# Causal mask of forgetting attention: added to the scores by a matrix product in PSUM instead of read from masked forget sums

## The reference, cut to what matters

```python
def fox_block(q, k, v, fq, fk, qpos, kpos):
    logits = jnp.einsum('bhqd,bhkd->bhqk', q, k).astype(jnp.float32) * (q.shape[-1] ** -0.5)
    logits = logits + fq[..., :, None] - fk[..., None, :]
    logits = jnp.where(qpos[:, None] >= kpos[None, :], logits, -jnp.inf)
    p = jax.nn.softmax(logits, axis=-1)
    return jnp.einsum('bhqk,bhkd->bhqd', p.astype(v.dtype), v)
...
fcum = jnp.cumsum(logf, axis=-1)   # fk: running sum of the log forget values
```

## Time and profile before

| | |
|---|---|
| median of 3 runs | 3345.48 us (3340.01, 3345.48, 3346.04) |
| profiled execution, its own time | 3339.98 us |
| its span, first to last instruction | 3338.2 us |
| PE busy | 3124.5 us, 94% |
| PEld, DVE, ACT, POOL busy | 85%, 42%, 30%, 28% |
| mean granted TensorE clock | 0.975 of full speed |
| the eight fox groups | four from 372 to 733 us, four from 2003 to 2371 us |

### The profile page before, as it was taken

How to read it: one execution, slowest core, us unless ns; L and a number is a source line. 1 busy time by engine, 2 the same in 40 slices (tenths; PEclk the granted TensorE clock), 3 DMA queues, 4 the chain that set the end, 5 groups by cost and what they waited for, 6 DMA issues and landing times. The chain is left out here.

```text
span 3338.2 us, 48224 instructions
## 1 busy us (share of the span) xinstructions
PE 3124.5 (94%) x20188; PEld 2853.0 (85%) x20188; DVE 1386.7 (42%) x2770; ACT 999.2 (30%) x1774; POOL 946.7 (28%) x536
## 2 busy tenths in 40 slices
PE   5899999999999999999989899999899999999996
PEld 2887877789999999999857787788799999999995
DVE  2412244455544463345152114444545354533532
ACT  3220433333334243221040223333324343331211
POOL 0121212215343443332111121221344352523320
PEclk9899999999999999999989999999999999999998
DMA  7112212212112121432432212222212121123334
GB/s 269 65 34 82 71 68 72 72 49 74 52 53 62 48 61 45 165 114 82 172 134 76 78 34 72 72 72 72 65 49 67 42 73 47 51 100 123 125 101 166
DMA packets 125560, 277.97 MB, mean 83 GB/s; under 512 B 44385, under 2 KB 64353, under 8 KB 124193
## 3 DMA queue, kind: packets, MB, share of 16 engines
q1 hardware_dynamic: 125344, 274.89, 24.3%
HBM read 217.24 MB, written 62.05 MB: 84 GB/s over the span
## 5 line engine op out<-in xcount | busy, mean ns | idle before, releaser
L272 PE MATMUL ps<-sb_h_split,sb_w_split 128*128 128x364 f32 (+1 forms) x3504 | 1232.9, 352 | 73.8 <-POOL sb_w_split L323 25.2
L273 PE MATMUL ps<-sb_h_split,sb_w_split 128*128 128x364 f32 (+1 forms) x3504 | 1163.5, 332 | 0.0
L274 PE MATMUL ps<-sb_h_split,sb_w_split 128*128 128x364 f32 (+1 forms) x3504 | 1162.7, 332 | 0.0
L272 PEld LDWEIGHTS ps<-sb_h_split,sb_w_split 128*128 128x128 f32 x3504 | 671.8, 192 | 104.6 <-issue 49.8
L273 PEld LDWEIGHTS ps<-sb_h_split,sb_w_split 128*128 128x128 f32 x3504 | 672.0, 192 | 6.5 <-issue 1.1
L274 PEld LDWEIGHTS ps<-sb_h_split,sb_w_split 128*128 128x128 f32 x3504 | 669.5, 191 | 0.0
L321 POOL CAST sb_w_split<-sb_w_raw 128x1024 fp32r<-128x1024 f32 x154 | 179.0, 1162 | 1710.8 <-PE ps L274 1630.1
L323 POOL TENSOR_TENSOR sb_w_split<-sb_w_raw,sb_w_split 128x1024 fp32r<-128x1024 f32 x154 | 387.1, 2514 | 12.3
L1444 PE MATMUL ps<-sb_delta 128*128 128x128 f32 x2160 | 263.0, 276 | 0.0
L1444 PEld LDWEIGHTS ps<-sb_delta 128*128 128x128 f32 x2160 | 258.4, 191 | 1.5
L1137 ACT ACTIVATE sb_fox<-sb_fox 128x128 f32<-128x128 f32 (+5 forms) x144 | 111.9, 777 | 328.0 <-DVE sb_fox L1172 327.7
(11 more groups left out here) (222 smaller groups left out, 4031.7 us busy)
## 6 DMA issues: line engine op xcount, KB each, us to landing
sb_w_raw<-in_wblk SPq DMA_DIRECT2D x158, 512.0 KB, 3.7
scratch_gates<-sb_spill SPq DMA_DIRECT2D x72, 182.0 KB, 1.9
sb_o_split<-scratch_o SPq DMA_DIRECT2D x24, 544.0 KB, 5.8
sb_fox<-scratch_fcum SPq DMA_DIRECT2D x8, 1600.0 KB, 6.7
sb_w_raw<-in_wbr SPq DMA_DIRECT2D x48, 256.0 KB, 3.9
sb_raw_qk<-scratch_gates SPq DMA_DIRECT2D x22, 544.0 KB, 3.7
sb_w_raw<-in_adaw SPq DMA_DIRECT2D x20, 512.0 KB, 15.8
sb_norm<-scratch_x SPq DMA_DIRECT2D x8, 1088.0 KB, 8.4
```

Of the source, the lines that this page charges most:

```text
L272: pe.matmul(out, w_hi, x_hi, start=first, stop=False)
L273: pe.matmul(out, w_hi, x_lo, start=False, stop=False)
L274: return pe.matmul(out, w_lo, x_hi, start=False, stop=last)
```

## The change

The mask now enters as one more product. The constant `causal` holds -8e30 for keys in the future, and after the scores of a tile are in PSUM, PE multiplies the identity by it and accumulates the result onto the diagonal block (times 0.125 it is -1e30). DVE then needs one operation for the whole row, with fk itself. POOL no longer makes fd.

```diff
-    causal = np.where(i[None, :] > i[:, None], 1e30, 0.0)
+    causal = np.where(i[None, :] > i[:, None], -8e30, 0.0)
...
             def _(pool):
-                pool.wait_ge(*hist_loaded(16))
-                for h in range(2):
-                    pool.tensor_tensor(fd[:, h, 0:8, :], Q4(fk[:, h, 0:SEQ]),
-                                       causal.unsqueeze(1).to_broadcast([P, 8, P]), ALU.add)\
-                        .then_inc(*level_mask.up(1))
-                    pool.tensor_tensor(fd[:, h, 8, 0:DEC], fk[:, h, SCAN_OFF:FKEYS], causal[:, 0:DEC],
-                                       ALU.add).then_inc(*level_mask.up(1))
                 split_blocks(pool, [3, 6, 9, 12])
...
-                                           kT[64 * h:64 * h + 64, lo + a:lo + a + w], start=True, stop=True)
+                                           kT[64 * h:64 * h + 64, lo + a:lo + a + w], start=True,
+                                           stop=(a + w < n))
+                    a, w = P * (len(blk) - 1), blk[-1][1]
+                    for h in range(2):
+                        r = 0 if t < 8 else DEC * h
+                        mm = pe.matmul(ps[0:rows, 2 * h + a // 512, a % 512:a % 512 + w],
+                                       ident[r:r + rows, r:r + rows], causal[r:r + rows, r:r + w],
+                                       start=False, stop=True)
                     mm.then_inc(*scores_pe.up(1))
...
-                    lo, w = blk[0][0], blk[-1][1]
-                    n = P * (len(blk) - 1)
+                    lo, n = blk[0][0], sum(b[1] for b in blk)
...
-                    if n:
-                        dve.tensor_tensor_reduce(out=lg[0:rows, s % 2, 0:n], in0=src[:, 0:n],
-                                                 in1=fk[0:rows, h, lo:lo + n], scale=0.125, scalar=-3e38,
-                                                 op0=ALU.subtract, op1=ALU.max,
-                                                 accum_out=mx[0:rows, s, 0:1])
-                    dve.tensor_tensor_reduce(out=lg[0:rows, s % 2, n:n + w], in0=src[:, n:n + w],
-                                             in1=fd[0:rows, h, t, 0:w], scale=0.125, scalar=-3e38,
+                    dve.tensor_tensor_reduce(out=lg[0:rows, s % 2, 0:n], in0=src[:, 0:n],
+                                             in1=fk[0:rows, h, lo:lo + n], scale=0.125, scalar=-3e38,
                                              op0=ALU.subtract, op1=ALU.max,
-                                             accum_out=mx[0:rows, s, 1:2]).then_inc(*logits.up(1))
+                                             accum_out=mx[0:rows, s, 0:1]).then_inc(*logits.up(1))
                     dve.wait_ge(*logits(s + 1))
-                    other = mx[0:rows, s, 0:1] if n else mx[0:rows, s, 1:2]
-                    dve.tensor_scalar(mx[0:rows, s, 2:3], mx[0:rows, s, 1:2], other, -1.0,
-                                      ALU.max, ALU.mult).then_inc(*exps.up(1))
+                    dve.tensor_scalar(mx[0:rows, s, 2:3], mx[0:rows, s, 0:1], -1.0, None, ALU.mult)\
+                        .then_inc(*exps.up(1))
...
                 dve.wait_ge(*hist_loaded(16))
-                dve.wait_ge(*level_mask(4))
                 maxima(0)
```

More of the change, by code:

```diff
@@ L967, in fox_group @@
             at += 2 * FKEYS
-            fd = work[:, at:at + 2 * 9 * P].rearrange("p (h t c) -> p h t c", h=2, t=9)
-            at += 18 * P
             lg = work[:, at:at + 2048].rearrange("p (b c) -> p b c", b=2)
```

## The result

The changed kernel is slower: 3375.9 us (median of 4 runs, 3374.8 to 3378.4) against 3345.8 for the kernel before (4 runs, 3340.0 to 3346.1), a ratio of 1.0095 with a 95% interval of 1.0078 to 1.0113. The forecast was 3364, its own range 3357 to 3371. The direction held, but the change is 1.5 times what I had said (+30.1 us for +20), and the time lies above that range. It is inside the wider 3353 to 3376, which takes in rivals B and D, by 0.1 us; that is luck, since 7 of the changed kernel's 12 runs in this document are above 3376.

The account below looks back on a forecast made before the run. PE, busy 94% of the span, was taken to bound the kernel. Products +28.7, group starts -5.8 and clock -2.8 gave +20.1 us, from the runs' mean of 3343.8 to 3364 us; own range 3357 to 3371.

Parts of the forecast that it names:

- B: Rival: the gains at the groups' starts and the clock's reappear as waits elsewhere; +28.7 us, 3372.5; chance 15%.
- D: Rival: a gap behind the scores absorbs part of each tile, or DVE's saving counts; 3352 to 3356; chance 10%.
- the wider 3353 to 3376: The forecast's own range extended by D below and B above.
- What bounds the groups: Fox groups: PE bounds them; work added to PE costs its full length, savings elsewhere only the PE wait they end.
- DVE's 11 us: Maxima: one DVE operation instead of two saves 0.09 us per step, 11 us over 128 steps; taken as worth 0.
- The products, +28.7: PE's fp32 mask products: 0.429 us a tile over 64 tiles, 27.4 us, plus 1.2 for sample tiles; range 22 to 35.
- The starts of the groups, -5.8: PE's long waits for DVE's copies of v in groups 1, 5 and 6 shrink to 0.44 us; bounds 0 and -9.3.
- The clock, -2.8: Slow PE stretches behind the starts of groups 1 and 5 go, 1.29 + 1.50 us; bounds 0 and -5.
- A: Rival: weight loads aren't hidden, so mask products cost double, 0.86 us a tile, 57 us; 3393; chance 3%.
- C: Rival: products fit wholly into the gap behind the half-width scores, almost free; -8.6 us remain, 3335; chance 4%.
- The skill's rule: Transposes four times faster than fp32 products: a product would cost 0.42 us, the added term near 56; not adopted.

Follow-up runs that it names:

- e8: Changed kernel with the projection's fill placed eight steps ahead and ACT's places one step earlier; 3360.1 us, kernel before 3340.0 on that chip.
- e9: Kernel before with the first tile's fd made first and the fill eight steps ahead, no mask products; 3330.4 us, kernel before 3340.0.
- e2: Changed kernel without the mask's products, the mask left out altogether; 3336.9 us, -6.1 against the kernel before.
- e3: Kernel before with POOL making the first tile's fd first, in two small operations, no products; 3336.2 us, -6.9 against the kernel before.
- e1: Kernel before plus the mask's two fp32 products per tile, POOL's and DVE's work kept; 3369.0 us against 3343.1 before.
- e1b: The same kernel as e1 run again, on one chip with a2 and e12; 3370.7 us, kernel before 3340.4.
- a2: The changed kernel itself run again, on one chip with e1b and e12; 3371.5 us, kernel before 3340.4.
- e10: Changed kernel with the mask's products in bf16 and the fill eight steps ahead; 3329.6 us, kernel before 3340.0.
- e12: Changed kernel with the mask products issued twice in tiles 1 to 4; 3377.8 us, a2 3371.5 on the same chip.

## Why the prediction was wrong in its size

- **What bounds the groups**: right. PE's added length came through at an equal clock (e8 against e9, 29.7 us of 32.1), and no wait for the maxima or the exp appeared. DVE's 11 us were worth nothing that shows (e2 equal to e3).
- **The products, +28.7**: right in kind, 3.4 us short. The tile costs 0.49 us, not 0.43. The first fp32 products behind the half-width scores take 0.55 until the next instruction; the transposes behind them get 0.06 back. I had kept 3 to 6 us for just this and taken none. The sample tile gave 0.12 for my 0.16.
- **The starts of the groups, -5.8**: the amount was right to the tenth (9.3 to 3.5), in all of groups 1, 5 and 6, and so was the cause: POOL's order alone brings the same 3.5 (e3). What I hadn't seen is that the same wait also moves by itself with the time at which PE arrives: 4.0 and 6.6 us in two traces with the products and POOL untouched (e1, e1b). So e1 and e2 don't add up to the change.
- **The clock, -2.8**: this is the step that failed. I counted the two slow stretches that would go, behind the starts of groups 1 and 5, and they did go: 6.19 us in both, 5.70 and a mask pair. Of all other slow stretches I wrote only that they scatter by 3 us either way. In the profiled execution the term came out as 35.1 - 32.1 + 5.8 = +8.8, 11.6 us above mine, and the groups' ends alone, which I had put at nothing, account for +11.3. The mean clock of all runs fell from 0.974 to 0.970, which by the two slopes is 6 to 10 us. The groups end every 95.6 us (468.42, 564.06, 659.66), and behind all eight ends PE is slow for nearly 6 us, where before the same wait led to losses from 0.1 to 2.5 us. My own had groups at 0.98 and 0.96: that equal work ran at unequal clocks should have told me that a change of every group's length by some 4 us can redraw the slow stretches everywhere.
- **The range**: 3357 to 3371 is what the sum gives for products of 22 to 35 us; the clock's scatter of 3 us, which I name beside it, isn't in it. With it the range would have ended at 3373, still below what was measured.
- **Rival B**, the waits coming back elsewhere, gave 3372.5, the nearest figure, by the wrong mechanism: the waits stayed away. Rivals A, C and D are refuted by the 0.49 us a tile.
- **The skill's rule**: the Trainium skill ("TensorE: Matmul & The Clock Gate", Terms) has the transposition four times faster for FP32. Here four mask records, two products, take 0.45 to 0.55 us and seven transposes 0.68 to 0.74, so a product costs between two and three times a transposition; no run here shows four.

What stays open: why the clock is low behind the thin end of a group even where the 3.0 us wait is gone (e8, e9), what makes a dear end out of one distance between ends and a cheap one out of another, and what makes runs of one kernel differ, 0.968 to 0.973 in a2. A kernel whose groups keep their length but end with dense work wasn't tried, nor one that changes only the distance.

The fastest version is either of two, at 3330 us on a chip where the kernel before takes 3340: fd made first with the eight steps' lead (e9, ratio 0.9966, 0.9954 to 0.9979), or the mask as a bf16 product with the lead (e10, 0.9972, 0.9963 to 0.9981).

## What to carry to other kernels

Work moved onto the engine that is busy 94% of the time cost its full length here, and the type decided that length: the same mask is 0.49 us a tile in fp32 and 0.07 in bf16, where its two values are as good in either. A stall that a change removes may have a cheaper cure; here two small operations put first brought all of it. Before a wait is put down to an edit, look at whether it is the same in a second trace: this one was 4.0 us in one and 6.6 in another of the same kernel. And where stages repeat, a change of the stage's length can also change every later stretch of slow clock: put a range of several us on that, up and down, instead of counting only the stretches that go.

## What the runs showed that I had not expected

- A longer program can lose less to the clock: e12 has 14 us more work than the changed kernel and takes 6 us longer.
- The same wait of 3.00 us is followed by no slow stretch in one group and by one that costs 2.8 us in another, with the same work behind it.
- Two bf16 products of 128 columns take 0.12 us with their loads, less than half of what halving the fp32 records would give (0.27).
